# Weight parts of a split-precision matmul: two buffers one behind the other, or interleaved element by element

## The reference, cut to what matters

```python
for l in range(DEPTH):                                   # 2 layers, SEQ 512, D_MODEL 1024
    h = h + 0.5 * rms_norm(swiglu(rms_norm(h, g[0]), ffn1_gate[l], ffn1_up[l], ffn1_down[l]), g[1])
    m = hybrid_mixer(rms_norm(h, g[2]), w_in[l], ..., w_out[l], cos, sin)
    h = h + rms_norm(m, g[3])
    h = h + 0.5 * rms_norm(swiglu(rms_norm(h, g[4]), ffn2_gate[l], ffn2_up[l], ffn2_down[l]), g[5])

def swiglu(x, w_gate, w_up, w_down):                     # 1024 -> 2816 -> 1024
    return (jax.nn.silu(x @ w_gate) * (x @ w_up)) @ w_down
```

## Time and profile before

| | us |
|---|---|
| median of 3 runs | 1875.81 |
| lowest, highest | 1875.55, 1876.25 |
| the profiled execution | 1874.11 |
| its span in the trace | 1872.3 |

### The profile page before, as it was taken

How to read it: one execution, slowest core, us unless ns; L and a number is a source line. 1 busy time by engine, 2 the same in 40 slices (tenths; PEclk the granted TensorE clock), 3 DMA queues, 4 the chain that set the end, 5 groups by cost and what they waited for, 6 DMA issues and landing times.

```text
span 1872.3 us, 25256 instructions
## 1 busy us (share of the span) xinstructions
PE 1856.3 (99%) x9480; PEld 1534.4 (82%) x9480; DVE 986.5 (53%) x1350; ACT 710.3 (38%) x1115; POOL 202.3 (11%) x420
## 2 busy tenths in 40 slices
PE   9999999999999999999999999999999999999998
PEld 7888888888678888888888888889886888888887
DVE  6664433387757544432476544325877574444323
ACT  5333332255755333322253333223666453333321
POOL 3832000013100000000047200000130000000000
PEclk9999999999999999999999999999999999999999
DMA  6335343343223333343333443333511313333331
GB/s 197 101 103 146 95 119 93 85 144 102 57 68 91 98 93 101 95 121 94 100 93 99 108 132 113 107 95 104 161 51 53 113 57 101 93 98 114 97 93 45
DMA packets 332013, 188.61 MB, mean 101 GB/s; under 512 B 7028, under 2 KB 327512, under 8 KB 330904
## 3 DMA queue, kind: packets, MB, share of 16 engines
q1 hardware_dynamic: 325992, 168.60, 31.3%
q0 software_dynamic: 5824, 18.79, 3.3%
q10 hardware_dynamic: 112, 0.05, 0.0%
HBM read 175.72 MB, written 11.67 MB: 100 GB/s over the span
## 4 chain that ended last, share of the span: by engine, by line
PE 96%; DVE 2%; ACT 2%; issue 0%; DVEq 0%; ACTq 0%
PE ps L595 19%; PE ps L597 18%; PE ps L596 18%; PE ps L804 8%; PE ps L805 8%; PE ps L806 8%; PE ps L652 2%; PE ps L654 2%; PE ps L659 2%; PE ps L990 1%; PE ps L764 1%; PE ps L763 1%; PE ps L765 1%; PE ps L625 1%; PE ps L636 1%; PE ps L627 1%
## 5 line engine op out<-in xcount | busy, mean ns | idle before, releaser
L1677 DVE TENSOR_TENSOR wl<-raw,wh 128x1024 fp32r<-128x1024 f32 (+1 forms) x260 | 344.4, 1325 | 729.3 <-ACT wh L1175 728.0
L595 PE MATMUL ps<-xh,wh 128*128 128x512 f32 x1536 | 606.1, 395 | 2.2 <-ACT vc L1398 2.2
L597 PE MATMUL ps<-xh,wl 128*128 128x512 f32 x1536 | 598.2, 389 | 0.0
L596 PE MATMUL ps<-xl,wh 128*128 128x512 f32 x1536 | 597.9, 389 | 0.0
L1175 ACT ACTIVATE wh<-raw 128x1024 fp32r<-128x1024 f32 (+1 forms) x260 | 295.8, 1139 | 621.4 <-PE ps L806 324.6
L595 PEld LDWEIGHTS ps<-xh,wh 128*128 128x128 f32 x1536 | 288.4, 188 | 66.1 <-issue 4.8
L597 PEld LDWEIGHTS ps<-xh,wl 128*128 128x128 f32 x1536 | 288.3, 188 | 60.5
L596 PEld LDWEIGHTS ps<-xl,wh 128*128 128x128 f32 x1536 | 288.5, 188 | 60.0 <-issue 1.9
L804 PE MATMUL ps<-Hh,wh 128*128 128x512 f32 x638 | 248.4, 389 | 0.0
L806 PE MATMUL ps<-Hh,wl 128*128 128x512 f32 x638 | 248.2, 389 | 0.0
L805 PE MATMUL ps<-Hl,wh 128*128 128x512 f32 x638 | 248.2, 389 | 0.0
(11 more groups left out here) (390 smaller groups left out, 2020.0 us busy)
## 6 DMA issues: line engine op xcount, KB each, us to landing
raw<-in_ffn_gate SPq DMA_DIRECT2D x88, 512.0 KB, 3.8
raw<-in_ffn_up SPq DMA_DIRECT2D x88, 512.0 KB, 3.8
raw<-in_ffn_down SPq DMA_DIRECT2D x64, 704.0 KB, 4.5
raw<-in_w_in SPq DMA_DIRECT2D x28, 512.0 KB, 4.1
raw<-in_w_out SPq DMA_DIRECT2D x16, 512.0 KB, 3.6
xrow<-in_x SPq DMA_DIRECT2D x4, 512.0 KB, 7.2
ssm_t<-evict POOLq DMA_DIRECT2D x8, 256.0 KB, 3.6
ssm_v<-evict POOLq DMA_DIRECT2D x8, 256.0 KB, 3.5
```

The costliest lines, as they stand in the source:

```text
L595: pe.matmul(bank, w_tile(True, slot, kw), xh[:, kx, :], start=first, stop=False)
L596: pe.matmul(bank, w_tile(True, slot, kw), xl[:, kx, :], start=False, stop=False)
L597: return pe.matmul(bank, w_tile(False, slot, kw), xh[:, kx, :], start=False, stop=last)
L1677: V.tensor_tensor(w_low(slot, k0, nk), raw[:, slot4, 0:nk - k0, :], w_high(slot, k0, nk).bitcast(F32), ALU.subtract).then_inc(w_split, 1)
```

## The change

The high and the low tensor of each slot become one tensor with a last dimension of 2: element 0 is the high part, element 1 the low part of the same weight. So the elements of one part lie 8 bytes apart instead of 4, in what ACT writes, in what DVE reads (high) and writes (low), and in the stationary operand that PE loads. `raw` and the activations keep their layout. The interleaved tensor is as large as the two before it, and lies where they lay.

```diff
-        wh = sb("wh", [P, SPLIT_SLOTS, KH, P], F32R)
-        wl = sb("wl", [P, SPLIT_SLOTS, KH, P], F32R)
+        whl = sb("whl", [P, SPLIT_SLOTS, KH, P, 2], F32R)
         with ExitStack() as alias:
-            whx = alias.enter_context(nc.sbuf_tensor("whx", [P, KD, P], F32R))
-            wlx = alias.enter_context(nc.sbuf_tensor("wlx", [P, KD, P], F32R))
+            whlx = alias.enter_context(nc.sbuf_tensor("whlx", [P, KD, P, 2], F32R))
...
+        def w_part(slot, k, part):
+            return whl[:, slot, k, :, part] if slot < SPLIT_SLOTS else (whlx, whlq, whlr, whlf)[slot - SPLIT_SLOTS][:, k, :, part]
+
         def w_high(slot, k0, k1):
-            return wh[:, slot, k0:k1, :] if slot < SPLIT_SLOTS else (whx, whq, whr, whf)[slot - SPLIT_SLOTS][:, k0:k1, :]
+            return w_part(slot, slice(k0, k1), 0)
 
         def w_low(slot, k0, k1):
-            return wl[:, slot, k0:k1, :] if slot < SPLIT_SLOTS else (wlx, wlq, wlr, wlf)[slot - SPLIT_SLOTS][:, k0:k1, :]
+            return w_part(slot, slice(k0, k1), 1)
 
         def w_tile(high, slot, k):
-            return (w_high if high else w_low)(slot, k, k + 1).rearrange("p a n -> p (a n)")
+            return w_part(slot, k, 0 if high else 1)
...
-                    pe.matmul(bank, wh[:, slot, k, :], Hh[:, f, cols_h], start=(f == 0), stop=False, skip_group_check=True)
+                    pe.matmul(bank, w_tile(True, slot, k), Hh[:, f, cols_h], start=(f == 0), stop=False, skip_group_check=True)
```

More of the change, by code:

```diff
@@ L286, in build @@
         with ExitStack() as alias:
-            whq = alias.enter_context(nc.sbuf_tensor("whq", [P, KD, P], F32R))
-            wlq = alias.enter_context(nc.sbuf_tensor("wlq", [P, KD, P], F32R))
+            whlq = alias.enter_context(nc.sbuf_tensor("whlq", [P, KD, P, 2], F32R))
         qa = sb("qa", [P, SWA_PAIRS, SEQ])
@@ L294, in build @@
         with ExitStack() as alias:
-            whf = alias.enter_context(nc.sbuf_tensor("whf", [P, KD, P], F32R))
-            wlf = alias.enter_context(nc.sbuf_tensor("wlf", [P, KD, P], F32R))
+            whlf = alias.enter_context(nc.sbuf_tensor("whlf", [P, KD, P, 2], F32R))
         qf = sb("qf", [P, FOX_HEADS, SEQ])
@@ L313, in build @@
         with ExitStack() as alias:
-            whr = alias.enter_context(nc.sbuf_tensor("whr", [P, KD, P], F32R))
-            wlr = alias.enter_context(nc.sbuf_tensor("wlr", [P, KD, P], F32R))
+            whlr = alias.enter_context(nc.sbuf_tensor("whlr", [P, KD, P, 2], F32R))
         rot = sb("rot", [P, 4, SEQ])
@@ L762, in half_products @@
                     bank = ps[b][:, cols_h]
-                    pe.matmul(bank, wh[:, slot, k, :], Hh[:, f, cols_h], start=(f == 0), stop=False, skip_group_check=True)
-                    pe.matmul(bank, wh[:, slot, k, :], Hl[:, f, cols_h], start=False, stop=False, skip_group_check=True)
-                    return pe.matmul(bank, wl[:, slot, k, :], Hh[:, f, cols_h], start=False, stop=(f == KF - 1),
+                    pe.matmul(bank, w_tile(True, slot, k), Hh[:, f, cols_h], start=(f == 0), stop=False, skip_group_check=True)
+                    pe.matmul(bank, w_tile(True, slot, k), Hl[:, f, cols_h], start=False, stop=False, skip_group_check=True)
+                    return pe.matmul(bank, w_tile(False, slot, k), Hh[:, f, cols_h], start=False, stop=(f == KF - 1),
                                      skip_group_check=True)
@@ L803, in down_pair @@
                             f = (i % 2) * KH + k
-                            pe.matmul(bank, wh[:, slot, k, :], Hh[:, f, :], start=(f == 0), stop=False)
-                            pe.matmul(bank, wh[:, slot, k, :], Hl[:, f, :], start=False, stop=False)
-                            mm = pe.matmul(bank, wl[:, slot, k, :], Hh[:, f, :], start=False, stop=(f == KF - 1))
+                            pe.matmul(bank, w_tile(True, slot, k), Hh[:, f, :], start=(f == 0), stop=False)
+                            pe.matmul(bank, w_tile(True, slot, k), Hl[:, f, :], start=False, stop=False)
+                            mm = pe.matmul(bank, w_tile(False, slot, k), Hh[:, f, :], start=False, stop=(f == KF - 1))
                         mm.then_inc(unit_done, 1)
```

## The result

| | us | against before |
|---|---|---|
| before, median | 1875.84 | |
| after, median (1919.73 to 1920.9) | 1920.17 | 1.0241, 95% interval 1.0229 to 1.0253 |
| after, span of the profiled execution | 1918.3 | +46.0 on 1872.3 |

The account below looks back on a forecast made before the run. PE was taken as the bound, paced by its moving operand. Weight loads, ACT's high parts, DVE's low parts and memory each added 0, leaving the median at 1875.8 us; the 8-in-10 range was 1871 to 1925.

Parts of the forecast that it names:

- What bounds it: Whole kernel: PE, busy 99% of the span, with the moving operand setting the distance between matmul starts.
- feel nothing until 226.7 ns: PE's 6522 and a few more 512-column matmuls: no cost unless the load's own pace passes 226.7 ns.
- the 12.7 ns behind the moving columns: Part of each matmul interval on PE taken as independent of the columns, from 226.7 ns at 512 and 119.7 at 256.
- The load itself: PE's spaced weight loads: 113.4 ns pace expected to stay, cost 0; 852 matmuls with 256 columns exposed beyond 119.7 ns.
- lower bound: PE's spaced load: same 1024-byte stretch as 256 moving columns, so 107 ns suffice, below 113.4; cost 0.
- upper bound from L2120: PE's spaced load: DVE's 0.867 ns per spaced element on 128 columns, 224.4 ns pace, +89 us over 852 matmuls.
- The signs: What the new profile would show: 256-column distance above 119.7 ns means B; 512-column above 226.7 means E, below it D.
- rival E: PE's weight load passes 226.7 ns: 7.4 us per ns, +800 us at twice C's price per element; chance 0.02.
- Rival B: Weight load becomes the pace of PE's 256-column matmuls: 0 to +89 us, in the middle +42, 1918 us; chance 0.18.
- Rival D: PE faster: the unexplained 12.7 ns shrink by 1 ns on some 7400 matmuls, -7.4 us, 1868 us; chance 0.04.
- Rival C: ACT and DVE pay L2120's full price on the splits, exposed in the mixer: +20 us, 1895 us; chance 0.14.
- strict reading of the second half: PE's load crosses 64 memory lines instead of 32, 0.867 ns for each more: 141.1 ns pace, +18 us.

Follow-up runs that it names:

- e9: Kernel before, contiguous weight tiles, but 120 of 128 weight columns loaded in most matmuls with 512 moving columns; 1915.12 us, ratio 1.0214.
- m1: Matmuls alone in runs of 24, no kernel, stationary spacing and moving columns varied; 512 columns: 226.7 ns at spacing 1, 233.8 at 2.
- e4: Kernel before, but PE loads every fourth element of four neighbouring tiles, 16 bytes apart; 2032.66 us, ratio 1.0839.
- e2: Changed kernel, ACT and DVE still writing interleaved, but PE loads 128 neighbouring elements of the tile pair; 1876.64 us, ratio 1.0006.
- e3: Kernel before, but PE loads every second element of two neighbouring tiles for the low parts only, one matmul in three; 1902.51 us, ratio 1.0147.

## Why the prediction was wrong

- *What bounds it* was right: PE's pace, no wait.
- *The step that failed* is the sentence that the 512-column matmuls "feel nothing until 226.7 ns" of load pace. It took the 12.7 ns behind the moving columns for a constant, read from two sizes with one kind of load. It is not one: the distance less columns / 2.4 GHz is 13.3 ns at 512 columns with a contiguous load, 20 ns with a spaced one (233.3 - 213.3), and 20 ns also with a contiguous one of 120 columns (e9). The load's own pace went to 117.5 ns, far below 226.7, and yet 7014 matmuls paid 6.6 ns. They are also more than the prediction's "6522 and a few more", which left out 492 in the other slots.
- *The load itself.* Taken as 0, measured as some +6 ns (111.8 to 117.5, m1), which still fits under the 119.7 ns of the 256-column matmuls; the prediction had named a rise to just under that as the way to be right about these for a wrong reason. Its lower bound held there, since those matmuls did not move; the upper bound from L2120, 224.4 ns, is near what spacing 4 and 8 cost (233.8 and 241.3 ns with 256 columns), and far from spacing 2.
- *The signs.* The prediction put a distance above 226.7 ns down to rival E, a load slower than that. The distance rose and E is false: the load takes 117.5 ns.
- *Rival B* came out right in size (+42) by chance: its mechanism did not happen, as the 120.0 ns show. It does at spacing 4 (e4). The end of the range at 1925 was drawn through it and C, so that the time lies inside the range for a wrong reason.
- *Rival D* named the unexplained 12.7 ns and priced them at 7.4 us per ns, but only as a gain. The loss is this term with the other sign: 7014 x 6.6 ns.
- *Rival C* fell: DVE pays nothing, ACT 73 ns of the 888 priced, and e2 shows them hidden.
- *The Trainium skill* ("SBUF — State Buffer", section "Door 1: The DMA port swizzle"), by which two hits on a 16-byte line keep full bandwidth and each crossing pays: the first half agrees for DVE (1219 ns at spacing 1 and 2, 2009 at 4), and nearly for the load (+6 ns) and ACT (+57 ns). The prediction's strict reading of the second half, 141.1 ns for the load, does not agree: 117.5.

Why the gap takes steps is not shown. That it depends on the number of moving columns, on the number of weight columns and on their spacing is. That it does so through the time of the load is not: with 512 moving columns the contiguous loads of 64, 96, 112, 120 and 128 columns give 230.0, 230.0, 229.6, 233.3 and 226.7 to 227.5 ns, in no order of size, and no run shows how long a load of 120 or 112 columns takes by itself. Many of the paces (120.0, 146.7, 160.0, 173.3, 226.7, 233.3 ns) are whole multiples of 6.67 ns, and the toll is one such step; others (203.3, 225.4, 229.6) are not. A fixed beat under it is an inference from that.

## What to carry to other kernels

Where PE runs back to back, read the distance of two matmul starts less columns / 2.4 GHz before changing anything that touches the stationary operand: a few ns there are multiplied by every matmul, however well the load seems to be hidden. Keep the stationary tile contiguous and 128 columns wide, or measure the pair of sizes; and do not trust that a smaller matmul is a quicker one. A layout for ACT and DVE may space float32 elements by 8 bytes at little cost, by 16 bytes at double.

## What was not expected of the hardware

- A contiguous load of 120 columns gives a slower stream (233.3 ns) than one of 128 (226.7 to 227.5), with the same 512 moving columns; 508 moving columns (227.5) are no quicker than 512. Of all loads measured beside 512 columns, none gives a quicker stream than the contiguous one of 128.
- One spaced load in three slows all three matmuls: 231.1 ns in the mean (e3).
- Spacing 4 doubles the load's pace, 111.8 to 233.8 ns for 128 columns; spacing 8 adds little more (241.3 ns with 256 moving columns).
- The gap is gone at TensorE's lower clock. In m1, during line 115 (128 moving columns, loads at spacing 4), the granted clock falls from 1.00 to 0.50, the lower of the two levels, and stays there from 101.3 to 111.2 us. There seven matmuls of 320 contiguous columns take 110.46 - 108.59 = 1.87 us, 267 ns each, which is 320 / 1.2 GHz with nothing left; at the upper clock 320 columns take 146.7 ns, 13.3 more than 320 / 2.4 GHz. The spaced loads did not slow down with the clock: at spacing 8 the pace is 240.0 ns at 0.50 (128 moving columns) and 241.3 at 1.00 (256).
